# A Winograd-form down projection: a fourth split slot, a new item order, one sum left to an adding DMA, and four quads in both chunk pairs

## What is computed

```python
def swiglu(x, w_gate, w_up, w_down):
    return (jax.nn.silu(x @ w_gate) * (x @ w_up)) @ w_down
...
h = layer_norm(ALPHA * h + 0.5 * swiglu(h, ffn1_w_gate, ffn1_w_up, ffn1_w_down), ln1_g, ln1_b)
mix = hybrid_mixer(h, ...)
h = layer_norm(ALPHA * h + mix, ln2_g, ln2_b)
h = layer_norm(ALPHA * h + 0.5 * swiglu(h, ffn2_w_gate, ffn2_w_up, ffn2_w_down), ln3_g, ln3_b)
```

## Time and profile before

| | |
|---|---|
| median of three runs | 1941.09 us |
| profiled execution | 1941.81 us, of which the span from first to last instruction is 1939.8 us |
| TensorE (PE) busy | 1909.5 us, 98% |
| DVE busy | 1253.9 us, 65% |
| ACT busy | 894.1 us, 46% |
| DMA | 357.37 MB, 184 GB/s in the mean |

### The profile page before, as it was taken

How to read it: one execution, slowest core, us unless ns; L and a number is a source line. 1 busy time by engine, 2 the same in 40 slices (tenths; PEclk the granted TensorE clock), 3 DMA queues, 4 the chain that set the end, 5 groups by cost and what they waited for, 6 DMA issues and landing times.

```text
span 1939.8 us, 27987 instructions
## 1 busy us (share of the span) xinstructions
PE 1909.5 (98%) x10490; PEld 1617.4 (83%) x10490; DVE 1253.9 (65%) x1411; ACT 894.1 (46%) x996; POOL 66.9 (3%) x93
## 2 busy tenths in 40 slices
PE   9999999999999999999999999999999999999997
PEld 8888888888778778999999888888888888877776
DVE  5555554555887887676766958555554555587887
ACT  5444443444454553545644544444444444455452
POOL 0000000000000001300131000000000000000000
PEclk9999999999999999999999999999999999999999
DMA  8666666667565665655442067566666666545654
GB/s 304 193 187 189 189 185 189 178 193 235 157 211 182 214 219 171 212 181 161 127 133 89 23 225 243 171 186 182 186 190 197 192 187 188 189 163 184 206 190 168
DMA packets 185365, 357.37 MB, mean 184 GB/s; under 512 B 11328, under 2 KB 23616, under 8 KB 184272
## 3 DMA queue, kind: packets, MB, share of 16 engines
q1 hardware_dynamic: 183600, 347.43, 57.4%
q0 software_dynamic: 1696, 8.99, 1.4%
HBM read 354.28 MB, written 2.10 MB: 184 GB/s over the span
## 4 chain that ended last, share of the span: by engine, by line
PE 91%; DVE 5%; issue 1%; DMA 1%; ACT 1%; POOL 0%; POOLq 0%; SPq 0%; DVEq 0%; ACTq 0%
PE acc L463 23%; PE acc L465 23%; PE acc L464 23%; PE acc L486 3%; PE acc L488 3%; PE acc L490 3%; PE tp L985 1%; PE tp L987 1%; PE tp L986 1%; DVE wlo L451 1%; PE tp L917 1%; PE acc L985 1%; PE acc L987 1%; PE acc L986 1%; ACT whi L444 1%
## 5 line engine op out<-in xcount | busy, mean ns | idle before, releaser
L451 DVE TENSOR_TENSOR wlo<-raw,whi 128x1024 fp32r<-128x1024 f32 (+2 forms) x579 | 692.5, 1202 | 602.8 <-ACT whi L444 600.7
L444 ACT ACTIVATE whi<-raw 128x1024 fp32r<-128x1024 f32 (+2 forms) x579 | 596.6, 1037 | 815.3 <-PE acc L465 726.9
L463 PE MATMUL acc<-whi,xT 128*128 128x512 f32 (+2 forms) x1644 | 631.0, 384 | 0.8 <-ACT zab L1612 0.4
L465 PE MATMUL acc<-whi,xT 128*128 128x512 f32 (+2 forms) x1644 | 625.7, 381 | 0.0
L464 PE MATMUL acc<-wlo,xT 128*128 128x512 f32 (+2 forms) x1644 | 625.2, 380 | 0.0
L463 PEld LDWEIGHTS acc<-whi,xT 128*128 128x128 f32 x1644 | 308.7, 188 | 64.7 <-issue 1.8
L465 PEld LDWEIGHTS acc<-whi,xT 128*128 128x128 f32 x1644 | 308.7, 188 | 59.5
L464 PEld LDWEIGHTS acc<-wlo,xT 128*128 128x128 f32 x1644 | 308.9, 188 | 55.8
L463 PE MATMUL acc<-whi,hT 128*128 128x512 f32 x432 | 170.8, 395 | 6.7 <-DVE wlo L451 6.7
L464 PE MATMUL acc<-wlo,hT 128*128 128x512 f32 x432 | 168.4, 390 | 0.0
L465 PE MATMUL acc<-whi,hT 128*128 128x512 f32 x432 | 168.4, 390 | 0.0
(11 more groups left out here) (345 smaller groups left out, 1854.6 us busy)
## 6 DMA issues: line engine op xcount, KB each, us to landing
raw<-in_ffn_w_down_dram SPq DMA_DIRECT2D x176, 512.0 KB, 4.7
raw<-in_ffn_w_up_dram SPq DMA_DIRECT2D x175, 512.0 KB, 3.7
raw<-in_ffn_w_gate_dram SPq DMA_DIRECT2D x174, 512.0 KB, 3.8
raw<-in_w_in_dram SPq DMA_DIRECT2D x48, 512.0 KB, 3.9
raw<-in_w_out_dram SPq DMA_DIRECT2D x32, 512.0 KB, 6.4
raw<-in_w_in_dram SPq DMA_DIRECT2D x32, 260.0 KB, 2.8
raw<-in_w_in_dram SPq DMA_DIRECT2D x16, 456.0 KB, 5.2
raw<-in_w_q_idx_dram SPq DMA_DIRECT2D x8, 512.0 KB, 3.8
```

Of the source, the lines that this page charges most:

```text
L444: act.activation(hi[:, s, :, 0:w], raw[:, r, :, 0:w], ACT.Copy).then_inc(hi_done, 1)
L451: dve.tensor_tensor(lo[:, s, :, 0:w], raw[:, r, :, 0:w], hi[:, s, :, 0:w].bitcast(F32), ALU.subtract).then_inc(lo_done, 1)
L463: pe.matmul(o, hi, w_hi[:, s, k, 0:width], start=first and k == 0, stop=False)
L465: ins = pe.matmul(o, lo, w_hi[:, s, k, 0:width], start=False, stop=last and k == UNIT_KT - 1)
```

## The change

Four things change, all of them in the two down stages.

- **Quads.** Both pairs have four quads. Pair 0 has a head of 13 plain units, two plain units in each quad and a tail of 7; pair 1 a head of 2, four in each quad, and 10 behind the last form's group.
- **Order.** A group's forms come as P1, P3, P5, then P7, P6, then P2, P4, with plain units between, so a group of pair 0 is: unit, P1, P3, P5, unit, P7, P6, P2, P4, and one of pair 1: unit, P1, P3, P5, unit, P7, P6, unit, P2, P4, unit. The raws are ordered to suit. The sums change sign, so that each is an addition; P6's goes into the slot of the block (a, 0), P5's and P4's share one buffer `form_sum`. DVE makes the sum for an item two items ahead of it. The token side's sums are spread over items 2 to 14 of pair 0, where they were in items 2 to 9 before.
- **The adding DMA.** P7's sum isn't made by DVE any more. GpSimd issues a DMA (`down_pool`) that reads block (b, 1) from DRAM once more and adds it to block (a, 1) in its `raw` slot. It waits until P5's sum, which reads that block, is made. ACT's split for P7 waits for `right_added`.
- **Slots.** The two buffers that this frees are a fourth slot for high and low parts, in use from item 16 of pair 0 on (the first P5) to the edge units. `split_slots` hands the slots out in the order in which they were last used, so nothing is turned round any more.

The folds are the same work in 8 steps for 7, with the last two in one item and with signs changed.

```diff
@@ -63,13 +63,13 @@
...
-            self.raws += [(a, 0), (a, 1), some[0], (b, 1), some[1], (b, 0), *some[2:]]
-            forms = [("P1", "P5"), ("P7", "P3"), ("P6", "P2"), ("P4",)]
+            self.raws += [some[0], (a, 0), (b, 1), (a, 1), *some[1:3], (b, 0), *some[3:]]
+            forms = [("P1", "P3", "P5"), ("P7", "P6"), ("P2", "P4"), ()]
             for k in range(4):
                 if k < len(some):
                     self.items.append(("unit", *some[k]))
                 self.items += [(form, q, 0) for form in forms[k]]
-        self.tail = len(self.items)
+        self.tail = 1 + max(i for i, item in enumerate(self.items) if item[0] == "P4")
         plain(len(units))
         self.quads = quads
@@ -85,12 +85,22 @@
...
 
     def released_by(self, r):
 
-        return max(i for i, (what, _, _) in enumerate(self.items)
-                   if what not in ("P4", "P5", "P6") and self.raw_of(i) == r)
+        last = max(i for i, (what, _, _) in enumerate(self.items)
+                   if what not in ("P4", "P5") and self.raw_of(i) == r)
+        for q, (a, b) in enumerate(self.quads):
+            if self.raws[r] in ((a, 0), (b, 0)):
+                return max(last, self.item("P4", q) - 1)
+            if self.raws[r] == (b, 1):
+                return max(last, self.item("P6", q) - 1)
+        return last
 
@@ -101,6 +111,22 @@
...
+
+def split_slots(pairs, one_more_from, kept_apart):
+
+
+    free, places = list(range(SPLIT_SLOTS)), [{}, {}]
+    user = {}
+    for pair, plan in enumerate(pairs):
+        for i in range(len(plan.items) - (kept_apart if pair else 0)):
+            if (pair, i) == (0, one_more_from):
+                free.insert(0, SPLIT_SLOTS)
+            s = free.pop(0)
+            free.append(s)
+            places[pair][i] = s, user.get(s)
+            user[s] = pair, i
+    return places, user
 
 
@@ -205,8 +231,10 @@
...
     ENDS = [*range(4), *range(12, DOWN_U)]
-    PAIRS = [Pair(QUADS[:3], sorted(ENDS + [7, 11]), sorted(ENDS + [7, 11]), 10, (4, 4, 4)),
-             Pair(QUADS, ENDS, ENDS, 2, (4, 4, 4, 3))]
+    PAIRS = [Pair(QUADS, ENDS, ENDS, 13, (2, 2, 2, 2)),
+             Pair(QUADS, ENDS, ENDS, 2, (4, 4, 4, 4))]
+    FOURTH_FROM = 16
+    SPLITS, LAST_USER = split_slots(PAIRS, FOURTH_FROM, EDGES)
@@ -259,6 +287,9 @@
...
+        form_sum = mz("form_sum", 88, [P, UNIT_KT, BANK])
+        fourth_hi = mz("fourth_hi", 92, [P, 1, UNIT_KT, BANK], F32R)
+        fourth_lo = mz("fourth_lo", 96, [P, 1, UNIT_KT, BANK], F32R)
@@ -401,6 +432,17 @@
...
                 return edge_hi, edge_lo, slot, st.index(p, 0, edge_free(slot))
+            if plan_of(p) is not None:
+                f, pair = (0, 1)[p in DOWN[1]], (0, 1)[p in (F1DB, F2DB)]
+                s, before = SPLITS[pair][u] if u < n else (u - n, LAST_USER[u - n])
+                if before is not None:
+                    free = st.index(DOWN[f][before[0]], 0, before[1] + 1)
+                elif s < SPLIT_SLOTS:
+                    last = [v for v in range(2 * KU) if ring_place(v, 2 * KU, SPLIT_SLOTS) == s][-1]
+                    free = st.index(GU[f], GATE_CHUNKS - 1, last + 1)
+                else:
+                    free = None
+                return (whi, wlo, s, free) if s < SPLIT_SLOTS else (fourth_hi, fourth_lo, 0, free)
@@ -858,9 +900,10 @@
...
+        FOLDS = 8
         DOWN_SCALE = 0.25 / ALPHA
-        MADE = {"P5": 1, "P7": 2, "P6": 3, "P4": 4}
+        MADE = {"P5": 1, "P6": 2, "P4": 3}
@@ -880,11 +923,31 @@
...
+
+            pair = DOWN[f].index(p)
+            quads = [len(plan.quads) for plan in PAIRS]
+            return 16 * (sum(quads) * f + sum(quads[:pair]) + q + 1)
+
+        def down_pool(pool, f, w_down):
+
+            down_v = w_down.rearrange("(k p) n -> p k n", p=P)
+            for pair, p in enumerate(DOWN[f]):
+                plan = PAIRS[pair]
+                for q, (a, b) in enumerate(plan.quads):
+                    right = raw_ready(pool, p, a, 1)
+                    pool.wait_ge(sem("formed"), made(f, p, "P5", q))
+                    if right_added(f, p, q) > 16:
+                        pool.wait_ge(sem("right_added"), right_added(f, p, q) - 16)
+                    col = (2 * pair + 1) * BANK
+                    pool.dma_start(right, down_v[:, 2 * b:2 * b + 2, col:col + BANK], accum_op=ALU.add)\
+                        .then_inc(sem("right_added"), 16)
 
         def p_free(f, pair):
@@ -1045,12 +1107,17 @@
...
-                if name in MADE:
+                if name == "P7":
+                    act.wait_ge(sem("right_added"), right_added(f, p, q))
+                elif name in MADE:
                     act.wait_ge(sem("formed"), made(f, p, name, q))
                 else:
                     v = raw_unit(p, i)
                     act.wait_ge(raw_loaded[v % RAW_SLOTS], st.loaded(p, 0, v))
-                act.wait_ge(unit_used, free)
+                if free is None:
+                    act.wait_ge(sem("formed"), summed(f, "S4 low"))
+                else:
+                    act.wait_ge(unit_used, free)
                 act.activation(w_hi[:, s], form_raw(p, i), ACT.Copy).then_inc(hi_done, 1)
@@ -1145,26 +1213,28 @@
...
 
-                first = p == DOWN[f][0] and q == 0
-                a, b = plan_of(p).quads[q]
+                pair, plan = DOWN[f].index(p), plan_of(p)
+                a, b = plan.quads[q]
+                corner = raw_ready(dve, p, a, 0)
                 if name == "P5":
-                    upper, left = raw_ready(dve, p, a, 1), raw_ready(dve, p, a, 0)
-                    if first:
-                        dve.wait_ge(sem("formed"), summed(f, "S4 low"))
-                    elif q == 0:
-                        dve.wait_ge(sem("formed"), folded(f, 0, FOLDS))
-                    dve.tensor_tensor(sumB[:, 0], upper, left, ALU.subtract).then_inc(sem("formed"), 1)
-                if name == "P7":
-                    block, right = raw_ready(dve, p, b, 1), raw_ready(dve, p, a, 1)
-                    dve.tensor_tensor(right, block, right, ALU.subtract).then_inc(sem("formed"), 1)
+                    upper = raw_ready(dve, p, a, 1)
+                    if q > 0:
+                        dve.wait_ge(lo_done, st.index(p, 0, plan.item("P4", q - 1) + 1))
+                        dve.wait_ge(hi_done, st.index(p, 0, plan.item("P4", q - 1) + 1))
+                    else:
+                        dve.wait_ge(sem("formed"), folded(f, 0, FOLDS) if pair else summed(f, "S4 low"))
+                    dve.tensor_tensor(form_sum[:], upper, corner, ALU.add).then_inc(sem("formed"), 1)
                 if name == "P6":
+                    block = raw_ready(dve, p, b, 1)
+                    dve.wait_ge(lo_done, st.index(p, 0, plan.item("P1", q) + 1))
+                    dve.wait_ge(hi_done, st.index(p, 0, plan.item("P1", q) + 1))
                     dve.wait_ge(sem("formed"), made(f, p, "P5", q))
-                    dve.tensor_tensor(sumB[:, 1], raw_ready(dve, p, b, 1), sumB[:, 0], ALU.subtract)\
-                       .then_inc(sem("formed"), 1)
+                    dve.tensor_tensor(corner, block, form_sum[:], ALU.add).then_inc(sem("formed"), 1)
                 if name == "P4":
                     left = raw_ready(dve, p, b, 0)
+                    dve.wait_ge(lo_done, st.index(p, 0, plan.item("P5", q) + 1))
                     dve.wait_ge(sem("formed"), made(f, p, "P6", q))
-                    dve.tensor_tensor(sumB[:, 2], left, sumB[:, 1], ALU.subtract).then_inc(sem("formed"), 1)
+                    dve.tensor_tensor(form_sum[:], left, corner, ALU.add).then_inc(sem("formed"), 1)
@@ -1286,22 +1365,15 @@
...
-                    what, q, _ = plan.items[i]
-                    after = plan.items[i + 1] if i + 1 < len(plan.items) else ("", 0, 0)
-                    if after[0] == "P1":
-                        add(p, "P5", after[1])
-                    if what == "P5":
-                        add(p, "P7", q)
-                    if what == "P7":
-                        add(p, "P6", q)
-                    if after[0] == "P6":
-                        add(p, "P4", after[1])
-                    if what == "unit":
+                    if plan.items[i][0] == "unit":
                         split_lo(dve, p, 0, i)
                     else:
                         form_lo(p, i)
                     if pair == 0:
                         sums(i)
+                    soon, of, _ = plan.items[min(i + 2, len(plan.items) - 1)]
+                    if soon in MADE:
+                        add(p, soon, of)
                     if i >= plan.tail:
                         pair_end(pair, i - plan.tail)
@@ -2654,10 +2726,12 @@
...
+            down_pool(pool, 0, ffn1_w_down[0])
             pool.wait_ge(unit_used, gains_free(0))
             norm_gains(pool, ln1_g, ln1_b)
             norm_pool(pool, 0)
             mixer_pool(pool)
+            down_pool(pool, 1, ffn2_w_down[0])
```

(51 more changed lines are left out.)

39 lines of the change are left out of this document (16 added, 23 removed).

## The result

| | before | after |
|---|---|---|
| median | 1941.88 us (4 runs) | 1979.19 us (4 runs, 1975.82 to 1983.67) |
| ratio, 95% interval | | 1.0194 [1.0171, 1.0217] |
| profiled execution | 1941.81 us | 1977.84 us |
| forecast | | 1934 us, range 1922 to 1957 |

Each ratio in this text is against executions of the kernel before that were measured together with the kernel in question (their medians lie between 1941.88 and 1943.46 us).

A forecast was written before the change was run, and what follows sets the result against it. PE, busy 98%, was taken as the bound, so fewer matmuls or gaps win time. Quads -2.7, slots and order -17.0, adding DMA +12.8 sum to -6.9 us on 1941.8; median forecast 1934 us, range 1922 to 1957.

The forecast's parts named there:

- What L is: Passage estimating L for the adding DMA: least 3.5 us, 4.5 plain, 5.9 with a second read, up to 8.5.
- L: Time from the end of P5's sum to `right_added`, the adding DMA's landing, in each quad of the down stages.
- L = 5.9: Chosen L for the adding DMA: 4.5 us for a plain load with semaphore plus 1.4 for the second read.
- the term +12.8 us: Loss from the adding DMA in pair 0 of both down stages: 8 x (5.9 - 4.3).
- the prediction's own formula: Each of pair 0's eight quads in both down stages loses L - 4.3 us when L is above 4.3.
- The loop: Pair 0, from one quad's P5 sum through the adding DMA to the next: 10.65 us + L, against PE's 14.96.
- A loss only above L = 7.5: Pair 1: two more low parts make 12.9 us + L against PE's 20.4, so no loss up to L = 7.5.
- Item 4: The forecast's part on the adding DMA: the wait for it and the next (a, 1) load, +12.8 us in all.
- PE's 12 matmuls: One more quad in pair 0 of each down stage saves 6 matmuls a stage: -2.7 us.
- the gaps of before, -17.0: PE's gaps hanging on the splits in both down stages, all to be removed by slots and order: -17.0 us.
- the two terms' -19.7: Gain in the down stages before the adding DMA's cost: -2.7 us from quads and -17.0 from slots and order.
- a rival with chance 0.3: Adding DMA as new bound: slower from L = 6.8, by over 0.2% from 7.2; 1963 us at 8.5; chance 0.3.

The follow-up runs named there:

- the plain copy's run: The changed kernel with GpSimd's DMA copying block (b, 1) over the slot, without the addition: 1960.97 us, one run.
- the run with the filled waits: The changed kernel with eight zero matmuls ahead of PE's wait at P7, in all quads but pair 1's first: 1977.93 us, ratio 1.0188.

## Why the prediction was wrong

**The step that failed** is the last of "What L is": the choice of L = 5.9, and with it the term +12.8 us. In the four quads of pair 0 in the first stage, the end of P5's sum and the landing lie 6.8, 8.0, 9.5 and 7.7 us apart (534.33 to 541.15 is the first), 8.0 in the mean; in the second stage they lie 6.5, 8.6, 9.9 and 9.2 apart, and all eight 8.3 in the mean. By the prediction's own formula 8 x (8.3 - 4.3) = 32 us, beside the 30.2 that pair 0 cost. The loop was the right one and L was 2.4 us too small. The formula isn't exact: from landing to the end of the next sum there were 11.1 to 11.7 us for its 10.65, since the load of (a, 1) took 3.5 to 4.6 us for the 3.4 that it had. Of the 2.4 us in L, the plain transfer is the larger part. From issue it was taken as 4.4, between GpSimd's loads of before; here it took 6.5 in the median. And 0.5 us pass between the end of the sum and the instruction, for which L had 0.1. The addition itself was put at 1.4 us, and the plain copy's run shows 0.8. The Trainium skill's rule of two source reads, in "Collectives: The Full Stack", section "The bandwidth ceiling: the fold count and why AG ≠ RS ≠ AR", is measured there on a reduction between cores. It pointed the right way; no halving is seen here, since the addition made 6.5 us into 7.3.

**Pair 1.** "A loss only above L = 7.5" failed for another reason. L was 6.7 to 8.7 there, 7.8 in the mean, which by that sentence is 8 x 0.3 = 2.4 us; 23.3 were measured. The 12.9 us beside L were pair 0's 10.65 and two more low parts; 15.6 to 16.3 were measured. Item 4 had counted the load of (a, 1) for pair 0, at the 3.4 us of the fastest load of before, and no raw load for pair 1. There it comes third in a burst of six and takes 6.4 to 7.2, and P1's block in the same burst was late too. With (a, 1) loaded earlier 14.4 to 15.3 us were left, so (a, 1) alone isn't it; in the quad whose rows stand above, the wait that began with P1's block is 1.9 of the 2.7 us. The periods of 22.4 to 24.3 us against 20.4 give 2.0 + 3.0 + 3.9 = 8.9 us in the first stage and, from the issues at 1843.66, 1866.31, 1891.07 and 1915.06, 10.2 in the second: 19.1 of the 23.3.

**What was right.** PE's 12 matmuls; the gaps of before, -17.0: with P7 in a place where the DMA delays nobody, the ledger has 19.6 us before and 2.6 after, 17.0 less, and the two terms' -19.7 stand beside 1920.78 - 1941.81 = -21.0 measured in the profiled executions. That the 17.0 comes out to the tenth is luck: the forecast gave it to another order, and with P7 in the middle and DVE's sums 8.4 of the 19.6 us stay. The place of the waits at P7 in pair 0 and the mechanism, an adding DMA as the new bound, were foreseen as a rival with chance 0.3 and the point L = 7.2; only its 1963 us at L = 8.5 fell short, mainly by pair 1.

**What was not foreseen.** That the fourth quad in pair 0 brings nothing while DVE makes four sums, and that without the fourth slot nothing is gained. The prediction had credited slots and order together. A fourth slot in the order of before wasn't run, so whether it needs the new order isn't known. What stays open: why the clock fell behind some waits and not behind others (2.21 us at 543.61 and slow steps behind it, 3.26 at 712.47 and none). It decides nothing here, by the run with the filled waits.

## What to carry to other kernels

Work that is moved off a busy engine to a DMA is free only if nothing in an in-order queue stands behind it: count what waits behind the consumer, and put the consumer as late in the order as the buffers allow. The same DMA cost 53 us where its consumer P7 stood ahead of P6, P2 and P4, and perhaps gained some 2 us behind them.

When a wait closes a loop (sum, DMA, split, release, load, next sum), add up every way round it, the loads included and at the durations that they have in bursts. Shortening one way gains no more than its distance to the next longest, here under 1 us a quad, and that can be lost again elsewhere in the loop; and filling an engine's idle time, or giving it back its clock, shows nothing while it isn't on the loop.

## What the runs showed of the hardware

- A plain GpSimd DMA of 512 KB from DRAM, with SP's loads beside it, landed 6.5 us after its issue in the median of 16; with the addition 7.3 us (5.9 to 9.3). The instruction takes 0.74 and 1.22 us in the mean, and starts some 0.5 us after the semaphore that releases it.
- After a wait of 2.2 to 4.3 us in an otherwise unbroken row of matmuls, TensorE's granted clock fell from its upper level towards 1.2 GHz behind 8 of the 14 long waits, for 7 to 9 steps of 0.43 us (0.76 in the window around one), and came back.
